# Stick-breaking attention: where VectorE's scans and differences stand in a step

## The reference

```python
z = jnp.einsum('bhqd,bhkd->bhqk', qb, kf) * scale
past = key_pos[None, :] < q_pos[:, None]
log_keep = jnp.where(past, jax.nn.log_sigmoid(-z), 0.0)
after = lax.cumsum(log_keep, axis=3, reverse=True) - log_keep
w = jnp.where(past, jnp.exp(jax.nn.log_sigmoid(z) + after), 0.0)
return jnp.einsum('bhqk,bhkd->bhqd', w.astype(v.dtype), v)
```

## Time and profile before

| | us |
|---|---|
| median of 3 runs | 2706.57 |
| lowest, highest | 2705.76, 2708.16 |
| the profiled execution, its own time | 2711.82 |
| its span | 2710.0 |
| TensorE busy | 2545.8 (94%) |
| VectorE busy | 1146.5 (42%) |
| ScalarE busy | 1055.7 (39%) |
| GpSimd busy | 831.8 (31%) |

### The profile page before, as it was taken

One profiled execution on the slowest core, in us unless ns is written; L12 is line 12 of the kernel. 1 busy time (PEld: TensorE's weight loads), 2 busy tenths in 40 slices (PEclk: granted clock), 3 DMA queues, 4 the chain that ended last, 5 costly groups with the idle time before them and its releaser, 6 DMA issues.

```text
span 2710.0 us, 41462 instructions
## 1 busy us (share of the span) xinstructions
PE 2545.8 (94%) x16510; PEld 2091.9 (77%) x16510; DVE 1146.5 (42%) x2009; ACT 1055.7 (39%) x2157; POOL 831.8 (31%) x538
## 2 busy tenths in 40 slices
PE   8999999999978888889999989999999999999999
PEld 6877787888755555556988779999999887778877
DVE  7856874332241111113356651323357776412212
ACT  5446555532222211124355644332234555532231
POOL 1004654212310322101311016654531110464563
PEclk9999999999989999999999989999999999999999
DMA  4232222333289999995311112323322111233331
GB/s 144 83 89 78 94 62 72 101 93 94 59 354 402 426 426 426 427 423 214 102 48 56 40 39 72 101 78 91 98 86 63 48 48 40 69 87 95 99 101 62
DMA packets 314193, 378.78 MB, mean 140 GB/s; under 512 B 10496, under 2 KB 284160, under 8 KB 289424
## 3 DMA queue, kind: packets, MB, share of 16 engines
q1 hardware_dynamic: 312848, 371.91, 39.2%
q0 software_dynamic: 1152, 4.19, 0.4%
HBM read 371.81 MB, written 4.26 MB: 139 GB/s over the span
## 4 chain that ended last, share of the span: by engine, by line
PE 67%; DMA 12%; DVE 9%; ACT 5%; POOL 3%; issue 3%; SPq 0%; ACTq 0%; DVEq 0%; POOLq 0%
DMA early<-in_w_up_e 11%; PE bank L2490 5%; PE bank L1984 5%; PE bank L2491 5%; PE bank L2492 5%; PE bank L2997 4%; PE bank L2998 4%; PE bank L2999 4%; PE bank L443 4%; PE bank L445 4%; PE bank L444 4%; POOL split L2465 2%; DVE early L684 2%; PE bank L3267 1%; PE bank L861 1%
## 5 line engine op out<-in xcount | busy, mean ns | idle before, releaser
L2465 POOL TENSOR_TENSOR split<-keep,split 128x1024 fp32r<-128x1024 f32 x143 | 350.5, 2456 | 450.8 <-ACT split L2439 450.8
L2490 PE MATMUL bank<-x_hi,split 128*128 128x264 f32 (+1 forms) x1280 | 397.7, 311 | 11.1 <-POOL split L2465 9.4
L2491 PE MATMUL bank<-x_lo,split 128*128 128x264 f32 (+1 forms) x1280 | 390.5, 305 | 0.0
L2492 PE MATMUL bank<-x_hi,split 128*128 128x264 f32 (+1 forms) x1280 | 390.2, 305 | 0.0
L2439 ACT ACTIVATE split<-keep 128x1024 fp32r<-128x1024 f32 x192 | 200.2, 1050 | 223.2 <-PE bank L2999 207.9
L1984 PE MATMUL bank<-early 128*64 128x256 f32 x2048 | 238.0, 386 | 37.0 <-DMA early<-in_w_up_e 30.0
L2490 PEld LDWEIGHTS bank<-x_hi,split 128*128 128x128 f32 x1280 | 241.4, 189 | 32.5 <-issue 19.0
L1984 PEld LDWEIGHTS bank<-early 128*64 128x64 f32 x2048 | 166.1, 139 | 119.6 <-issue 70.4
L2491 PEld LDWEIGHTS bank<-x_lo,split 128*128 128x128 f32 x1280 | 241.5, 189 | 9.9 <-issue 0.2
L2492 PEld LDWEIGHTS bank<-x_hi,split 128*128 128x128 f32 x1280 | 240.5, 188 | 10.3
L3035 DVE TENSOR_TENSOR mlp<-mlp,bank 128x264 f32<-128x264 f32 (+1 forms) x96 | 49.5, 516 | 326.5 <-ACT mlp L3014 326.5
(11 more groups left out here) (490 smaller groups left out, 6072.9 us busy)
## 6 DMA issues: line engine op xcount, KB each, us to landing
early<-in_w_gate_e SPq DMA_DIRECT2D x64, 1024.0 KB, 10.9
early<-in_w_up_e SPq DMA_DIRECT2D x64, 1024.0 KB, 11.4
early<-in_w_down_e SPq DMA_DIRECT2D x64, 1024.0 KB, 10.9
early<-in_w_in SPq DMA_DIRECT2D x68, 512.0 KB, 3.7
keep<-in_mlp_w_in SPq DMA_DIRECT2D x64, 512.0 KB, 3.9
keep<-in_mlp_w_out SPq DMA_DIRECT2D x64, 512.0 KB, 3.7
keep<-in_a_w_qkv SPq DMA_DIRECT2D x24, 512.0 KB, 3.8
early<-decay_rows SPq DMA_DIRECT2D x16, 512.0 KB, 3.7
```

The source lines that it names most:

```text
L2465: e.tensor_tensor(lo, x, whole(hi), ALU.subtract).then_inc(*u.free(sig_, "lo", n))
L2490: e.matmul(o, hi[:, k, :], xh, start=k == 0, stop=False, skip_group_check=True)
L2491: e.matmul(o, hi[:, k, :], xl, start=False, stop=False, skip_group_check=True)
L2492: m = e.matmul(o, lo[:, k, :], xh, start=False, stop=k == 7, skip_group_check=True)
```

## The change

VectorE's part of a stick step is put in another order. Before, `stick_sums(e, i - 1)` stood between the scores of step i and the positive part of step i, and the last step's sums at the end. Now `stick_sums(e, i)` follows the positive part of the same step, ahead of the dense tile's splitting, scaling or adding back. The wait for TensorE's scores is kept only where VectorE copies the meta scores (t = 4); in the other steps VectorE waits for ScalarE's softplus alone.

```diff
                 if what == "z":
                     x = lanes(i)
-                    e.wait_ge(*SA.pe.to("z", i))
                     if STICK[i][1] == 4:
                         b = BR.of("zm", i)
+                        e.wait_ge(*SA.pe.to("z", i))
                         e.tensor_copy(ZM.take(i).ap, b.ap[:, 0:32]).then_inc(*b.free(SA.dve, "copied", i))
-                    if i > 0:
-                        stick_sums(e, i - 1)
                     e.wait_ge(*SA.act.to("soft", i))
                     for a, ks, z in read(i):
                         y = x[:, a, ks]
                         e.scalar_tensor_tensor(out=y, in0=z, scalar=0.0, in1=y, op0=ALU.max, op1=ALU.add).then_inc(*SA.dve.up("keep", i))
-                    if i == 35:
-                        stick_sums(e, i)
+                    stick_sums(e, i)
```

## The result

The changed kernel takes 2749.74 us (median of 4 runs, 2747.88 to 2750.07) against 2707.35 for the kernel before (4 runs, 2705.76 to 2708.16): ratio 1.0156, 95% interval 1.0138 to 1.0173, or 42 us slower, between 37 and 47. It was forecast at 2742, range 2728 to 2757.

A forecast was written before the change was run, and what follows sets the result against it. The prediction took TensorE's waits for single VectorE results, not VectorE's total work, as the bound in the stick-step stage. Its terms summed to 35.8 us, added to the median of 2706.6 for 2742 us, range 2728 to 2757.

The forecast's parts named there:

- Step 3 into 4: Sums and differences ahead of the scaling delay the scores of steps 4, 13 and 22 by 1.7 each: +5.2 us.
- GpSimd: GpSimd's subtraction meets the second scan at steps 12, 21 and 30: 0.6 us each, +1.8, bounds 0 and 5.4.
- Step 4 into 6: Later value scaling holds step 3's transposes 2.2 us, while step 6's scores stop waiting for differences: +3.8 us in three groups.
- the clock's term: TensorE at a lower clock behind its longer pauses, mostly ahead of steps 9, 18, 27 and 31: +6 us, bounds +1 and +14.
- Steps 7 to 9: The group's last value scaling and a copy come later, delaying scores of steps 9, 18 and 27: 4.5 each, +13.5 us.
- The copy's delay: Step 7's sums and differences hold the copy that lets ScalarE begin step 8's softplus: 0.6 us.
- Steps 27 to 35: Adding back of the output product comes later at steps 30, 31 and 34: 3.0, 1.4 and 2.3, +6.7 us.
- What it gives back: At steps 18 and 27 late differences no longer hold scaling and adding back: 0.4 and 0.8, -1.2 us.
- the one on the group's last scaling alone: Rival: slack covers the waits at steps 4, 6 and 31 to 35; 13.5 and the clock's 4 remain: 2724, chance 0.08.
- the faster one: Rival: earlier differences free score banks and transposes sooner, and the scaling is never waited for longer: 2701, chance 0.02.
- the one without effect: Rival: VectorE's idle pauses in the stage swallow the new order: within 5 us of 2706.6, chance 0.04.
- the heavy clock: Rival: pauses keep TensorE at 1.2 GHz over much of steps 4 to 9, scans held in full: 2754, chance 0.17.

The follow-up runs named there:

- e5: The changed kernel, with GpSimd's subtraction at steps 12, 21 and 30 held until VectorE finished that step's differences: 2743.62 us.
- e6: The changed kernel, with TensorE's pauses ahead of steps 4, 9, 13, 18, 22, 27, 31 and 35 filled by products nobody reads: 2741.87 us.
- e1: The changed kernel, but in steps 8, 17 and 26 the sums and differences stand behind the value scaling, as before: 2734.6 us.
- e2: The kernel before, with the new order of sums and differences in steps 8, 17 and 26 alone: 2721.11 us.
- e4: The changed kernel, but each step's sums and differences stand behind the dense tile's splitting, scaling or adding back everywhere (steps below 35): 2717.07 us.
- e9: As e4, but where the next step has meta scores to copy, the sums come right behind that copy: 2704.58 us, ratio 0.9987.

## Why the prediction was right

**The bound.** That TensorE's waits for VectorE decide and VectorE's load does not, held: VectorE's busy time in the stage is 163 us after and 166 before.

**Step 3 into 4** was 1.73; measured 1.6 in the first group. The others, 2.7 (2.9 of wait instead of 0.18), have GpSimd's share in them; in e5, without it, they are 1.65.

**Step 4 into 6.** The transposes' wait of 2.2 us came as 2.25, and the scores' 1.17 went. The three pieces grew by 7.3 us for 3.8 forecast, and the difference belongs to the clock's term: in the first group the transposes and scores ran at a low clock from 1378.3 on, in the other two the scores of steps 13 and 22, behind the pauses of 2.91, took 2.47 us for 1.32. In e6, with the pauses ahead of steps 4, 13 and 22 filled, the same three pieces grew by 1.24, 1.31 and 1.23, 3.8 in all. So the term's size was right, and what came on top is the clock.

**Steps 7 to 9,** the largest term, 4.5 a group: the scores of the next group came 4.4 us later at each, if the first group is taken from the scores of step 7 on (48.23 and 52.47 from the first scores). e1 and e2 bear it out from both sides: from the scores of step 8 to those of 9 it is 3.9 us more in e2, where the copy is not late, and 0.5 in e1, where only the copy is. The copy's delay, 0.6 in the prediction and a detail of that term, is the same mechanism that costs 11 us in e4, which I had not looked for.

**Steps 27 to 35:** 3.0, 1.4 and 2.3. The wait ahead of step 31 grew by 4.0 (1.80 to 5.78), of which GpSimd's share is 1.1: it is 2.9 in e5. The middle one came as 2.6, with slow products behind this longest pause, the last one as 2.3.

**What it gives back.** Behind step 27 0.6 us came back in the first trace, for 0.8; behind step 18 the piece grew by 0.95 instead of losing 0.4, and behind both pauses the clock was low. So this term is not borne out by itself.

**GpSimd** was taken at 0.6 for each of three steps with bounds 0 and 1.8, and measured 1.1 in the waits of e5, 3.3 in all. At step 30 GpSimd gets its turn between the two scans: the pair takes 2.93 us for 1.87. GpSimd's subtraction ends at 1584.46, and the second scan, 0.96 us long by itself, ends at 1585.30: it stood rather than ran slowly. The Trainium skill, GPSIMD Engine Reference, section Key points, says that GpSimd contends with VectorE instructions "with two SBUF inputs". For scans these traces agree with it.

**The clock** was taken at 6 us, bounds 1 and 14. The terms without clock as forecast, with GpSimd at its measured 3.3, sum to 31.3, so some 8 of the 38.9 us are left for it in the first trace, and by the same sum 13 of 44.6 in the second. Filling the pauses gave 4 in the median. The amount was near in the first trace, but the place was not, and there luck had a part. The prediction put 4.2 of its 6 us behind the three long pauses ahead of steps 9, 18 and 27. There the low stretch was hardly longer than before, since part of it fell into the pause: 3.9 us at 0.53 behind the one at step 9, for 3.7 us at 0.56 before the change. To the scores of the next step it was 0.1 us less at step 9, 0.95 more at 18, 0.6 less at 27 (1.0, 2.1 and 0.4 more in the second trace). What cost most in the first trace stood behind pauses of 2.4 to 2.9 us, which the prediction had called a little: the work from the scores of step 13 on took 8.71 us for 6.18, the same from step 22 on, and behind step 35 it was 1.6 more.

```profile
1405.09:1409.00 3.91, 3.91 (x33) 3.46 (x34) 1.24 (x12) 2.60 (x9) 0.22 (x1) 0.53 0.01 2
...
1443.16:1451.87 8.71, 8.71 (x49) 6.19 (x49) 2.63 (x7) 4.72 (x9) 0.47 (x1) 0.62 0.20 62
```

**The rest.** The median moved by 42.4, and 40.0 on the second chip, where the first pair of traces shows 37.9 in the span. The traced execution of the kernel before was 4.5 us slower than its own median, with a tail of 1103 us where the other thirteen traces have 1098 to 1101, and the second trace of the changed kernel has a stage 5.7 longer than the first. The prediction had named a change of over 2 us outside the stage as a sign that its account is wrong. The tail's 3 us are such a change, but they come from this one trace of the kernel before; the part ahead of the stage, which no experiment touches, lies between 1329.6 and 1334.5 us in the fourteen traces. The sum's error of 4 to 7 us is GpSimd's 1.5, the clock's 2 or more, and what differs from execution to execution. Of the rivals, the one on the group's last scaling alone is refuted by e1 (29 us are left without it), the faster one and the one without effect by the result; the heavy clock is neither: the medians, 40 and 42 us of growth, lie between the forecast's 36 and that rival's 47. GpSimd cost 3.3 us, between the forecast's 1.8 and that rival's 5.4, and the clock by the sums above 8 to 13, for 6 and 14.

## What to carry to other kernels

Where one engine's order is fixed and it shares a few banks, rank the work of the engine that frees them by what is waited for: first what frees a bank or lets a third engine begin (here a copy of 0.2 us), then what is needed two steps later. A pause of an engine that is half idle cost nothing by itself in e9; moving work out of it costs as much as that work then delays a release that somebody waits for. And a short wait taken away can come back a step later, so look for the next one before moving only one.

## What the runs showed of the hardware

A VectorE instruction with all operands in SBUF and a GpSimd subtraction took turns instead of overlapping: 0.18 us became 2.26, a pair of scans 1.87 became 2.93 and another 2.38 became 4.02, and GpSimd's own subtraction of 528 columns, 1.3 us at step 36, took 1.6 to 2.2 where VectorE had such work at the same time. Differences that read a bank ran beside it at their usual 1.28 us a pair (in the kernel before at 1468.47, beside a subtraction from 1468.48 to 1470.87).

The same program varied by 6 us in its stage from one execution to another, with mean granted clocks of 0.91 and 0.89, while the waits of the scores stood within 0.1 us. Low clock inside a pause cost nothing; low clock behind it did: the work that took 6.18 us at full clock took 8.71 at a mean of 0.62.
